# One TensorE tile shape for the attention scores of both layers, and another order of outputs and scores in layer one

## The reference

```python
# layer one
z = jnp.einsum('bhqd,bhkd->bhqk', q_blk, kf) * scale
log_stay = jnp.where(strict, jax.nn.log_sigmoid(-z), 0.0)
log_a = jax.nn.log_sigmoid(z) + lax.cumsum(after, axis=3, reverse=True)   # after: log_stay moved on by one
a = jnp.where(strict, jnp.exp(log_a), 0.0)
out = jnp.einsum('bhqk,bhkd->bhqd', a, vf)
# layer two, for each of three groups (window, dilation)
s = jnp.einsum('brhnqd,brhnkd->brhnqk', qb, kk) * scale + bias
p = jnp.exp(s - logsumexp(s))
```

## Time and profile before

| | |
|---|---|
| median of three runs | 766.65 us (766.53 to 766.77) |
| span of the profiled execution, first to last instruction | 765.1 us |
| TensorE busy | 756.2 us, 99% of the span |
| VectorE, ScalarE, GpSimd busy | 65%, 55%, 23% |
| mean traffic | 182 GB/s |

### The profile page before, as it was taken

The page is one execution under the profiler, slowest core; times in us unless marked ns, Lnnn a source line. Parts: engine busy times, 40 slices in busy tenths (PEclk is TensorE's granted clock), DMA queues, the critical chain, the costliest instruction groups (busy, mean ns, idle before and its releaser), DMA issues.

```text
span 765.1 us, 13561 instructions
## 1 busy us (share of the span) xinstructions
PE 756.2 (99%) x4731; PEld 651.5 (85%) x4731; DVE 493.7 (65%) x678; ACT 418.7 (55%) x633; POOL 172.6 (23%) x298
## 2 busy tenths in 40 slices
PE   9999999999999999999999999999999999999996
PEld 7999978888888888999899898898888888888884
DVE  5888987675455555777766667668547745544543
ACT  4766667453343343866875867767755444333421
POOL 1000001640000000236655765657302000000000
PEclk9999999999999999999999999999999999999998
DMA  8735675796654554559686786786744755566402
GB/s 246 211 117 153 209 230 165 232 272 201 209 193 164 176 194 123 162 158 236 158 217 157 180 215 167 164 224 204 202 138 147 267 196 188 172 215 209 171 1 55
DMA packets 160452, 139.62 MB, mean 182 GB/s; under 512 B 8217, under 2 KB 149121, under 8 KB 160417
## 3 DMA queue, kind: packets, MB, share of 16 engines
q1 hardware_dynamic: 153344, 131.45, 55.3%
q0 software_dynamic: 6784, 7.41, 5.4%
q10 hardware_dynamic: 288, 0.30, 0.2%
HBM read 138.02 MB, written 1.11 MB: 182 GB/s over the span
## 4 chain that ended last, share of the span: by engine, by line
PE 97%; DMA 1%; issue 1%; SPq 0%; POOL 0%; DVE 0%; DVEq 0%; POOLq 0%; ACT 0%
PE ps L1197 21%; PE ps L1199 20%; PE ps L1198 20%; PE ps L1447 10%; PE ps L1449 5%; PE ps L1203 3%; PE ps L1205 3%; PE ps L1204 3%; PE ps L1361 1%; PE ps L1510 1%; PE ps L1274 1%; PE ps L1291 1%; PE ps L1276 1%; PE ps L1277 1%; PE ps L1249 1%; PE ps L1475 1%
## 5 line engine op out<-in xcount | busy, mean ns | idle before, releaser
L805 DVE TENSOR_TENSOR w_lo<-raw,w_hi 128x2048 fp32r<-128x2048 f32 (+2 forms) x144 | 279.0, 1955 | 41.1 <-ACT w_hi L515 38.8
L515 ACT ACTIVATE w_hi<-raw 128x2048 fp32r<-128x2048 f32 (+2 forms) x144 | 232.8, 1637 | 57.1 <-DMA raw<-in_w_kv_b 25.7
L1197 PE MATMUL ps<-w_hi,xt 128*128 128x512 f32 x352 | 139.6, 396 | 0.0
L1199 PE MATMUL ps<-w_hi,xt 128*128 128x512 f32 x352 | 137.2, 390 | 0.0
L1198 PE MATMUL ps<-w_lo,xt 128*128 128x512 f32 x352 | 136.9, 389 | 0.0
L684 ACT ACTIVATE work<-ps,stat 128x256 f32<-128x256 f32 x44 | 21.0, 477 | 194.7 <-PE ps L1199 194.7
L425 POOL TENSOR_SCALAR stat<-stat 128x1 f32<-128x1 f32 x15 | 8.5, 566 | 443.6 <-ACT work L531 419.6
L1197 PE MATMUL ps<-w_hi,ot 128*128 128x512 f32 x240 | 94.8, 395 | 0.0
L1198 PE MATMUL ps<-w_lo,ot 128*128 128x512 f32 x240 | 93.5, 390 | 0.0
L1199 PE MATMUL ps<-w_hi,ot 128*128 128x512 f32 x240 | 93.5, 390 | 0.0
L1199 PEld LDWEIGHTS ps<-w_hi,xt 128*128 128x128 f32 x352 | 66.1, 188 | 14.1
(11 more groups left out here) (149 smaller groups left out, 1274.9 us busy)
## 6 DMA issues: line engine op xcount, KB each, us to landing
raw<-in_w_gate_up SPq DMA_DIRECT2D x88, 512.0 KB, 4.7
raw<-in_w_kv_b SPq DMA_DIRECT2D x96, 256.0 KB, 4.1
raw<-in_w_down SPq DMA_DIRECT2D x22, 1024.0 KB, 4.8
raw<-in_w_q_b SPq DMA_DIRECT2D x48, 256.0 KB, 4.2
raw<-in_w_qkv_a SPq DMA_DIRECT2D x23, 512.0 KB, 4.8
raw<-in_w_o_a SPq DMA_DIRECT2D x4, 1024.0 KB, 6.5
work<-bias_rows POOLq DMA_DIRECT2D x128, 32.0 KB, 3.6
raw<-in_w_o_b SPq DMA_DIRECT2D x4, 1024.0 KB, 5.1
```

The lines of the kernel that those rows point to most:

```text
L515: act.activation(w_hi[:, s % CUT, 0:size(s)], raw[:, s % RAW, 0:size(s)], ACT.Copy).then_inc(hi_made, 1)
L805: dve.tensor_tensor(w_lo[:, c, 0:n], raw[:, s % RAW, 0:n], w_hi[:, c, 0:n].bitcast(F32), ALU.subtract).then_inc(lo_made, 1)
L1197: mm(out, xs[0], ws[0], start=start, stop=False)
L1199: return mm(out, xs[1], ws[0], start=False, stop=stop)
```

## The change

In both layers the wide scores are formed with 32 stationary columns at a time. A block of 128 stationary columns becomes four of 32, each of which writes its own 32 partitions of the result; with the two heads that makes eight tiles of 64 rows by 32 columns. The moving operands are the same in size. 4 f32 matmuls of a pair become 16, in each layer. The waits of the scores are taken out into functions of their own (`scores_ready_a`, `scores_ready_b`), which are called ahead of the outputs. In layer one the outputs of pair p-2 now come before the scores of pair p-1; the first and the last pair's scores have no outputs beside them and stay where they are. In layer two the order of outputs and scores is as it was.

```diff
@@ -1249,14 +1249,18 @@
                     inst = mm(bank(0, SEQ * c, SEQ), first_w[c][:, k, :], xf[:, k, :], start=k == 0, stop=k == KT - 1)
                 inst.then_inc(first_used, 1)
 
-            def scores_a(a, j):
+            def scores_ready_a(a, j):
                 pe.wait_ge(qka_made, j * 2 + a + 1)
                 if a >= 1:
                     pe.wait_ge(arg_made, j * 2 + a)
-                for hh in range(2):
-                    rows_ = slice(DH * hh, DH * hh + DH)
-                    mm(bank(3 + hh, 0, SEQ), ka[rows_, 0:P], qa[rows_, :], start=True, stop=True)
-                    inst = mm(bank(3 + hh, SEQ, P), ka[rows_, P:SEQ], qa[rows_, P:SEQ], start=True, stop=True)
+
+            def scores_a(a):
+                for t in range(NT):
+                    for c in range(0, P, HR):
+                        for hh in range(2):
+                            rows_ = slice(DH * hh, DH * hh + DH)
+                            inst = mm(bank(3 + hh, SEQ * t, SEQ - P * t)[c:c + HR, :], ka[rows_, P * t + c:P * t + c + HR],
+                                      qa[rows_, P * t:SEQ], start=True, stop=True, skip_group_check=True)
                 inst.then_inc(z_done, 1)
 
             def values_a(h, j, ks=range(4)):
@@ -1308,9 +1312,10 @@
 
             def step_a(p, j):
 
-                scores_a(p - 1, j)
+                scores_ready_a(p - 1, j)
                 if p >= 2:
                     outputs_a(p - 2, j)
+                scores_a(p - 1)
                 project_a(p, j, 0, 0, 0)
                 project_a(p, j, 1, 0, SEQ)
                 sums_a(p - 1, j)
@@ -1467,13 +1472,17 @@
                 if t == 0 and k == KT - 1:
                     inst.then_inc(job_done, 1)
 
-            def scores_b(a, j):
+            def scores_ready_b(a, j):
+                pe.wait_ge(qkb_made, j * 12 + 6 * a + 3 if a else 2)
+
+            def scores_b(a):
                 heads = [slice(DH * hh, DH * hh + DH) for hh in range(2)]
 
                 def every(t):
-                    for hh, r in enumerate(heads):
-                        mm(bank(2 + 2 * hh + t, 0, P * (t + 1)), qb[r, 0, P * t:P * t + P], kb[r, 0, 0:P * (t + 1)],
-                           start=True, stop=True, skip_group_check=True)
+                    for c in range(0, P, HR):
+                        for hh, r in enumerate(heads):
+                            mm(bank(2 + 2 * hh + t, 0, P * (t + 1))[c:c + HR, :], qb[r, 0, P * t + c:P * t + c + HR],
+                               kb[r, 0, 0:P * (t + 1)], start=True, stop=True, skip_group_check=True)
 
                 def own(t, g):
 
@@ -1488,7 +1497,6 @@
                                       start=True, stop=True, skip_group_check=True)
                     return inst
 
-                pe.wait_ge(qkb_made, j * 12 + 6 * a + 3 if a else 2)
                 every(0)
                 every(1)
                 if not a:
@@ -1531,9 +1539,10 @@
 
             def step_b(p, j):
                 jj, a, before = j * 2, p - 1, j * 12 + 6 * (p - 1)
+                scores_ready_b(a, j)
                 if p >= 2:
                     outputs_b(a - 1, j)
-                scores_b(a, j)
+                scores_b(a)
                 pe.wait_ge(vb_made, j * 4 + 2 * p - 1)
                 wide_b(p, jj, 0, 0, 0).then_inc(block_done, 1)
                 pe.wait_ge(vb_made, j * 4 + 2 * p)
@@ -1579,7 +1588,8 @@
                start=True, stop=True).then_inc(bias_done, 1)
             values_a(0, 0)
             pe.wait_ge(bias_out_made, 1)
-            scores_a(0, 0)
+            scores_ready_a(0, 0)
+            scores_a(0)
             values_a(1, 0)
             pe.wait_ge(exact_made, 1)
             project_a(1, 0, 0, 0, 0)
@@ -1591,12 +1601,14 @@
                 step_a(3, j)
                 step_a(4, j)
             last = PAIRS - 1
-            scores_a(last - 1, 0)
+            scores_ready_a(last - 1, 0)
             outputs_a(last - 2, 0)
+            scores_a(last - 1)
             project_a(last, 0, 0, 0, 0)
             project_a(last, 0, 1, 0, SEQ)
             sums_a(last - 1, 0)
-            scores_a(last, 0)
+            scores_ready_a(last, 0)
+            scores_a(last)
             out_proj(WOA0, 0, 0, [0, 1, 2])
             outputs_a(last - 1, 0)
             out_proj(WOA0, 0, 0, [3])
@@ -1633,8 +1645,9 @@
             with pe.Fori(0, 3) as j:
                 step_b(2, j)
                 step_b(3, j)
+            scores_ready_b(PAIRS - 1, 0)
             outputs_b(PAIRS - 2, 0)
-            scores_b(PAIRS - 1, 0)
+            scores_b(PAIRS - 1)
             pe.wait_ge(vb_made, 2 * PAIRS - 1)
             out_proj(WOB0, PAIRS, 0, range(7), [0])
             pe.wait_ge(vb_made, 2 * PAIRS)
```

## The result

The changed kernel takes 770.79 us (four runs, 770.34 to 771.0) against 766.63 for the kernel before: a ratio of 1.0053, 95% interval 1.0039 to 1.0067. It is slower by 4.2 us, in the direction of the forecast and 0.9 us above the upper end of its range (764.6 to 769.9).

A forecast was written before the change was run, and what follows sets the result against it. PE was taken as the bound, with no idle time; layer one +3.15 us and layer two -1.6 gave +1.55, so 768.2, forecast as 768.3 us since the wait likelier costs more; range 764.6 to 769.9.

The forecast's parts named there:

- two waits: Layer one, PE: 0.49 us before the sums and 0.12 us before the outputs in each regular step.
- So the cover is 0.32 and the delay 0.77.: Layer one: scores reach ACT 0.77 us later, chain to the sums has 0.32 to spare; PE waits 0.49 per step.
- 3.97 + 0.05 = 4.02: 0.12 us: Layer one: outputs wait for DVE's masked weights until 4.02 after the sums' start; PE comes at 3.90, so waits 0.12.
- upper bound (0.18): Layer one: highest price of the outputs' wait for the mask, if it passes more slowly than the sums' wait.
- sixth step: Layer one, step before the last pair: sums already wait 0.19, so the new order costs 0.38 us in all.
- first and last pair: Layer one: their scores have no outputs ahead and save 0.04 us each.
- I take 0.20, since the feed fits: Layer two's scores: 0.20 us saved per pair, 1.6 over eight pairs, bounds 1.2 and 1.7.
- the shape change that goes: Layer two: wide scores take the small scores' tile shape, so 0.10 us for changing shape between them is saved.
- The covered chain: Rival, layer one: sums can take scores 0.77 later without waiting, leaving 1.9 us of gain; 764.7 us, chance 0.15.
- The smaller stalls: Rival, layer one: scores only 0.5 us late, sums wait about 0.2, layer one costs half; 766.7 us, chance 0.08.
- No difference to shape: Rival: tiles act as one wide tile, layer one +3.4, layer two 0; 770.0 us, chance within the main case's.
- Issue as the bound: Rival: feeding 12 more instructions in 16 blocks at 0.023 each adds 4.4 us; 772.7 us, chance 0.05.

The follow-up runs named there:

- shortened-exp kernel: Changed kernel with ACT's exp in layer one taken over 256 of 768 columns; 767.78 us, ratio 1.0011 to the kernel before.
- e6_chain_shorter: Changed kernel with ACT's exp and log in layer one both taken over 256 of 768 columns; 766.26 us, ratio 0.9993 to the kernel before.

## Why the prediction was right or wrong

**Right: what bounds, and the sign.** PE had no idle time, the order uncovered two waits in the six steps, and these outweigh what the tiles save. The experiments show it from both ends: order alone +4.7 us, tiles alone in both layers -1.2 (the two do not add up to the 4.2, since under the new order layer one's tiles bring nothing, and each time has its spread), and the step follows the length of the chain when that is changed.

**Wrong: "So the cover is 0.32 and the delay 0.77."** The mechanism was right, both sizes were off. The cover was taken from the chain's end to the sums' first matmul; it is their load that waits, and the load was issued 0.12 earlier, behind the projections' last matmul. The cover is 0.20, measured twice. The delay is 0.84 (1.83 less 0.99): 0.03 more in the outputs, whose first load is no longer issued ahead once PE has waited for the mask, and 0.04 more behind the scores, since ACT now starts 0.11 after the end of their record (59.46 to 59.57) and not 0.06; why is not known. From the step's start to the sums the change is +0.64 and not +0.45: 0.19 in each of six steps, 1.1 us.

**Wrong: "3.97 + 0.05 = 4.02: 0.12 us".** The outputs' load comes 0.12 after the mask and not 0.05, as the prediction had feared for its upper bound (0.18), and 0.18 it is: 0.06 six times, 0.4 us. There is also one step whose outputs are 0.13 longer (the second head starts 0.15 after the first; it is in the shortened-exp kernel too and was not explained), and two, the fifth and the sixth, in which ACT starts on the scores another 0.06 later, at 1.89. It stands idle until then; in the kernel before it has the same 0.06 in these two steps (1.05 instead of 0.99), where it cost nothing. With these, layer one costs 4.8 instead of 3.15.

| layer one | forecast | measured |
|---|---|---|
| from the outputs' load to the sums' load, five steps | 5 x 0.45 = 2.25 | 3.37 |
| the same, sixth step | 0.26 | 0.39 |
| wait for the mask, six times | 6 x 0.12 = 0.72 | 1.09 |
| first and last pair | -0.08 | -0.05 |
| sum | 3.15 | 4.8 |

**Wrong: "I take 0.20, since the feed fits".** The streams of the wide scores are as predicted (0.68 of 0.67), and so is the shape change that goes. The small matmuls behind them are limited by their number, which the prediction suspected as a limit of issue, and take back more of the gain than it allowed: 0.07 of 0.20, where a quarter was the bound. 8 x 0.13 = 1.07 us instead of 1.6.

So all three errors went the same way. They add 1.65 us in layer one and 0.5 in layer two, and with the 0.3 ahead of the first scores 1.55 became 4.1. The range took its upper end from the prices of single steps, without asking what all of them do together when they are wrong by what the rows' readings can be wrong by.

**The rivals.** The covered chain (0.15) is out: e6_chain_shorter shows what it would have looked like. The smaller stalls (0.08) are out: the scores came 0.84 late, not 0.5. No difference to shape (770.0) is nearest to the measured time, but by chance: layer two's 1.07 us did come, and layer one cost more than its 3.4; besides, its 770.0 lay above the range of which the prediction called it a part. Issue as the bound is out for the 16 wide matmuls; for the small ones it may hold in part. The Trainium skill, "TensorE: Matmul & The Clock Gate", section "Wait — 56ns, not 53.3ns?", gives about 62 ns for each matmul for the case that hardware decode is off. They do not show in this case: 16 wide and 32 small matmuls take 1.46 us in all, 0.030 each.

## What to carry to other kernels

When a block is moved ahead of another, add up the loop that runs through both, from engine to engine, and compare it with the bounding engine's own step; here 8.04 + 4.19 = 12.23 stood against 11.37, and no gain inside the blocks could show. Measure the cover of a wait to the first instruction that waits, on PE the load of the stationary operand and not the matmul. The gain of the finer tile shape was in loads and in a shape change here, not in streams, and it shrank where many short matmuls followed.

## What the runs showed of the hardware that I had not expected

- Eight tiles of 64 by 32 stream f32 at the rate of two of 64 by 128: the scores' slot, 768 columns over both passes, is 0.81 us against 0.86, and the difference is no more than the shorter loads can give.
- In the changed kernel's 32 short f32 matmuls behind 16 wide ones, the first records start 0.007 us apart and, after a pause of 0.11, most others 0.017. It hardly depends on what they stream: half the columns in 16 of 32 saved 0.02 to 0.05 us.
- After PE has waited for a semaphore of DVE, the first load came 0.05 us behind DVE's end at the sums and 0.12 at the outputs. The outputs have three waits in their function and the sums two; that this is the reason is not shown.
